# Two of a block's three split products as one product of 512 columns, and the halves added on VectorE

## What is computed

```
h = rmsnorm(x, g_mix)
(qa, ka, va, qb, kb, vb, qc, clat, iq, ik, iw, ga, gb, gc) = split(h @ w_in)
ya = swa_sink_attention(qa, ka, va)        # 16 heads
yb = moba_attention(qb, kb, vb)            # 8 heads
yc = dsa_attention(qc, rmsnorm(clat), ...) # 8 heads, 64 chosen keys
merged = (sigmoid(ga) * (ya @ w_br_a)
        + sigmoid(gb) * (yb @ w_br_b)
        + sigmoid(gc) * (yc @ w_br_c))
x = x + merged @ w_out
x = x + peer_ffn(rmsnorm(x, g_ffn), ...)
return rmsnorm(x, g_final)
```

## Time and profile before

| | |
|---|---|
| median of 3 runs | 2022.06 us (2021.14 to 2022.56) |
| profiled execution | 2017.58 us, its span 2016.3 us |
| TensorE matmul busy | 1781.4 us (88%) |
| VectorE busy | 1502.3 us (75%) |
| ScalarE busy | 924.2 us (46%) |
| GpSimd busy | 649.8 us (32%) |

### The profile page before, as it was taken

How to read it: one execution, slowest core, us unless ns; L and a number is a source line. 1 busy time by engine, 2 the same in 40 slices (tenths; PEclk the granted TensorE clock), 3 DMA queues, 4 the chain that set the end, 5 groups by cost and what they waited for, 6 DMA issues and landing times.

```text
span 2016.3 us, 28693 instructions
## 1 busy us (share of the span) xinstructions
PE 1781.4 (88%) x11068; PEld 1602.0 (79%) x11068; DVE 1502.3 (75%) x1986; ACT 924.2 (46%) x1474; POOL 649.8 (32%) x553
## 2 busy tenths in 40 slices
PE   6999999999999999957775244499999999999997
PEld 6999999999999887757775244488888888888886
DVE  4464444443466547998988899988988989999997
ACT  5444444444434441223443899843443443433443
POOL 1000000001035003467777677122222224435541
PEclk9999999999999999978988556799999999999999
DMA  9566565565555969999999999588999999999994
GB/s 312 172 173 170 164 173 171 165 176 164 159 168 201 341 208 416 371 419 402 417 412 419 371 389 400 212 333 350 407 415 386 401 398 398 403 414 404 403 407 193
DMA packets 293543, 627.88 MB, mean 311 GB/s; under 512 B 10364, under 2 KB 223405, under 8 KB 234958
## 3 DMA queue, kind: packets, MB, share of 16 engines
q0 software_dynamic: 48400, 343.95, 42.1%
q1 hardware_dynamic: 244414, 281.15, 40.6%
q10 hardware_dynamic: 640, 1.63, 0.2%
HBM read 622.45 MB, written 8.44 MB: 313 GB/s over the span
## 4 chain that ended last, share of the span: by engine, by line
PE 71%; DVE 10%; issue 5%; POOL 4%; ACT 4%; DMA 3%; DVEq 3%; POOLq 0%; ACTq 0%
PE ps L2043 34%; PE ps L1689 23%; DVE u_ring L1504 5%; PE ps L1885 4%; PE ps L1871 4%; DMA u_ring<-in_peer_u,idx_all 3%; DVEq L1454 3%; POOL u_ring L704 1%; POOL u_ring L713 1%; ACT ones L1141 1%; PE ps L1810 1%; PE ps L1791 1%; PE ps L2008 1%; POOL pick L723 1%; PE ps L1800 1%
## 5 line engine op out<-in xcount | busy, mean ns | idle before, releaser
L1263 DVE TENSOR_TENSOR w_lo<-raw,w_hi 128x2048 fp32r<-128x2048 f32 x111 | 256.8, 2313 | 319.4 <-ACT w_hi L787 319.4
L1689 PE MATMUL ps<-act_hi,w_hi 128*128 128x256 f32 x1520 | 436.9, 287 | 3.5 <-DVE act_lo L1387 2.9
L1689 PE MATMUL ps<-act_lo,w_hi 128*128 128x256 f32 x1520 | 430.8, 283 | 0.0
L1689 PE MATMUL ps<-act_hi,w_lo 128*128 128x256 f32 x1520 | 430.8, 283 | 0.0
L1198 ACT ACTIVATE v_hi<-v_raw 128x2048 fp32r<-128x2048 f32 x128 | 245.7, 1919 | 389.1 <-PE ps L2043 198.2
L2043 PE MATMUL ps<-v_hi,c_hi 128*128 128x512 f32 x1024 | 398.6, 389 | 1.2 <-DVE c_lo L1583 1.2
L2043 PE MATMUL ps<-v_lo,c_hi 128*128 128x512 f32 x1024 | 398.5, 389 | 0.0
L2043 PE MATMUL ps<-v_hi,c_lo 128*128 128x512 f32 x1024 | 398.5, 389 | 0.0
L1504 DVE CUSTOM_DVE_ANT_0 u_ring<-u_ring,ps 128x2048 f32<-128x2048 f32 x144 | 326.5, 2277 | 20.4 <-DMA u_ring<-in_peer_u,idx_all 20.1
L1579 DVE TENSOR_TENSOR v_lo<-v_raw,v_hi 128x2048 fp32r<-128x2048 f32 x128 | 293.2, 2291 | 53.2 <-ACT v_hi L1198 52.6
L787 ACT ACTIVATE w_hi<-raw 128x2048 fp32r<-128x2048 f32 x112 | 214.1, 1911 | 257.3 <-PE ps L1689 210.7
(11 more groups left out here) (253 smaller groups left out, 2297.8 us busy)
## 6 DMA issues: line engine op xcount, KB each, us to landing
v_raw<-in_peer_v SPq DMA_DIRECT2D x128, 1024.0 KB, 7.4
raw<-in_w_in SPq DMA_DIRECT2D x80, 1024.0 KB
raw<-in_w_out SPq DMA_DIRECT2D x16, 1024.0 KB
wq<-in_peer_w_q SPq DMA_DIRECT2D x8, 2048.0 KB, 13.3
raw<-in_w_br_a SPq DMA_DIRECT2D x16, 512.0 KB
bias_by_query<-bias_by_distance POOLq DMA_DIRECT2D x1, 4096.0 KB, 21.0
bias_st<-bias_by_query POOLq DMA_DIRECT2D x16, 256.0 KB, 4.7
raw<-in_w_br_b SPq DMA_DIRECT2D x16, 256.0 KB
```

What stands on the lines that cost most here:

```text
L1263: nc.vector.tensor_tensor(w_lo[:, j % NHL], raw[:, j % NRAW], w_hi[:, j % NHL].bitcast(F32), ALU.subtract).then_inc(lo_done, 1)
L1689: last = nc.tensor.matmul(out_ap, w_parts[wp][:, slot, k], act_parts[ap][:, k], start=(k == k0 and m == 0), stop=(k == k1 - 1 and m == 2))
```

## The change

High and low activations now lie in one tile `act_both` of shape [128, 2, 16, 256], and `act_hi` and `act_lo` are its halves. At each k the high weights multiply both halves in one matmul of 512 columns over a whole bank: its first 256 columns take high by high, its last 256 high by low. Low weights by high activations go, with 256 columns, into the first half. A block is 16 matmuls of 512 columns and 16 of 256. VectorE adds the halves of the bank: in the first stage and the bodies into a new tile `joined` (`join`), from which ScalarE then copies; in the merge the three sums of a block have a bank each (banks 0 to 2 or 3 to 5), and one `tensor_reduce` adds the halves of all three into `mtmp`, which one further instruction weights in place. TensorE now waits for `join_ok` in place of `evac_done`.

```
-                for m, (wp, ap) in enumerate(PRODUCTS):
-                    last = nc.tensor.matmul(out_ap, w_parts[wp][:, slot, k], act_parts[ap][:, k],
-                                            start=(k == k0 and m == 0), stop=(k == k1 - 1 and m == 2))
+            both, low_part = (w_hi[:, slot, k], act_both[:, :, k]), (w_lo[:, slot, k], act_hi[:, k])
+            pair = bank.rearrange("p (h t) -> p h t", h=2)
+            if k == k0:
+                nc.tensor.matmul(pair, *both, start=True, stop=False)
+                last = nc.tensor.matmul(bank[:, 0:T], *low_part, start=False, stop=False)
+            else:
+                nc.tensor.matmul(bank[:, 0:T], *low_part, start=False, stop=False)
+                last = nc.tensor.matmul(pair, *both, start=False, stop=(k == k1 - 1))
...
+        def join(n0, j):
+
+
+            dve.wait_ge(blk_done, n0 + (j + 1))
+            wait(dve, evac_done, n0 + (j - 1))
+            nc.vector.tensor_reduce(joined[:, j % 2], ps[:, J + j % 2].rearrange("p (h t) -> p t h", h=2), AX.X, ALU.add).then_inc(join_ok, 1)
...
-                act.wait_ge(blk_done, n0 + (j + 1))
-                nc.scalar.activation(gates[:, span(6 * T * b + T * (j - 2), T)], ps[:, J + j % 2, 0:T], ACT.Tanh,
+                act.wait_ge(join_ok, n0 + (j + 1))
+                nc.scalar.activation(gates[:, span(6 * T * b + T * (j - 2), T)], joined[:, j % 2], ACT.Tanh,
                                      scale=0.5).then_inc(evac_done, 1)
...
         for n in range(N_FIRST):
+            join(0, n)
             if n + 2 <= N_FIRST:
                 low(0, n + 2)
...
+            if not isinstance(b, int) or b > 0:
+                join(n0, -1)
             low(n0, 1)
+            join(n0, 0)
             low(n0, 2)
+            join(n0, 1)
             low(n0, 3)
             softmax(0)
+            join(n0, 2)
             low(n0, 4)
             softmax(1)
+            join(n0, 3)
             low(n0, 5)
+            join(n0, 4)
             low(n0, 6)
             outputs(0)
+            join(n0, 5)
             low(n0, 7)
             outputs(1)
+            join(n0, 6)
             low(n0, 8)
         dve.wait_ge(sink_in, 16)
         attention_bodies(dve, body)
+        join(N_BR, -1)
...
-                nc.vector.scalar_tensor_tensor(out=mtmp[:, j % 2, 0:2].rearrange("p g t -> p (g t)"), in0=gates[:, span(3 * T * m, 2 * T)],
-                                               scalar=1.0, in1=ps[:, J + j % 2, :], op0=ALU.add, op1=ALU.mult)
-                nc.vector.scalar_tensor_tensor(out=mtmp[:, j % 2, 2], in0=gates[:, span(3 * T * m + 2 * T, T)], scalar=1.0,
-                                               in1=ps[:, S_BANK + j % 2, 0:T], op0=ALU.add, op1=ALU.mult).then_inc(m_mul, 1)
+                nc.vector.tensor_reduce(mtmp[:, j % 2], ps[:, 3 * (j % 2):3 * (j % 2) + 3].rearrange("p g (h t) -> p g t h", h=2), AX.X, ALU.add)
+                dve.drain()
+                products = mtmp[:, j % 2].rearrange("p g t -> p (g t)")
+                nc.vector.scalar_tensor_tensor(out=products, in0=gates[:, span(3 * T * m, 3 * T)], scalar=1.0, in1=products,
+                                               op0=ALU.add, op1=ALU.mult).then_inc(m_mul, 1)
                 low(NRAW * i + N_BR, j + 2)
```

More of the change, by code:

```diff
@@ L230, in sem @@
         return ctx.enter_context(nc.semaphore(name))
-    act_hi = at("act_hi", 0, [P, NK, T], FR)
-    act_lo = at("act_lo", 16, [P, NK, T], FR)
+    act_both = at("act_both", 0, [P, 2, NK, T], FR)
+    act_hi, act_lo = act_both[:, 0], act_both[:, 1]
     w_hi = at("w_hi", 32, [P, NHL, NK, P], FR)
@@ L251, in build @@
     ident = at("ident", 204.5, [P, P])
+    joined = at("joined", 205, [P, 2, T])
     sinkb = at("sinkb", 207, [P, A_HEADS])
@@ L366, in build @@
     evac_done = sem("evac_done")
+    join_ok = sem("join_ok")
     SSQ = {0: 1, 1: 2, 2: 3, 4: 5, 5: 7}
@@ L839, in _ @@
                 high(0, n + 2)
-            bank = ps[:, J + n % 2]
+            bank = joined[:, n % 2]
+            act.wait_ge(join_ok, n + 1)
             if n in TURNED:
@@ L899, in queries @@
                 nc.scalar.activation(k_st[:, par], kT[:, span(key, T)], ACT.Copy)
-                act.wait_ge(blk_done, n0 + (par + 1))
-                nc.scalar.activation(q_st[:, par], ps[:, J + par, 0:T], ACT.Copy).then_inc(evac_done, 1)
+                act.wait_ge(join_ok, n0 + (par + 1))
+                nc.scalar.activation(q_st[:, par], joined[:, par], ACT.Copy).then_inc(evac_done, 1)
             def exps(par):
@@ L1681, in _, with wide_part, by_pairs @@
         w_wide = [w[:, :, :, :].rearrange("p s (a b) c -> p s a (b c)", b=WIDE // P) for w in w_parts]
-        def by_column(out_ap, slot, k0, k1, waits=None):
+        def wide_part(bank, slot, k, k0=0, k1=NK):
+            both, low_part = (w_hi[:, slot, k], act_both[:, :, k]), (w_lo[:, slot, k], act_hi[:, k])
[6 more added lines that the diff above has]
+                last = nc.tensor.matmul(pair, *both, start=False, stop=(k == k1 - 1))
+            return last
+        def by_pairs(bank, slot, k0=0, k1=NK, waits=None):
             for k in range(k0, k1):
@@ L1687, in by_column @@
                     waits(k)
-                for m, (wp, ap) in enumerate(PRODUCTS):
-                    last = nc.tensor.matmul(out_ap, w_parts[wp][:, slot, k], act_parts[ap][:, k],
-                                            start=(k == k0 and m == 0), stop=(k == k1 - 1 and m == 2))
+                last = wide_part(bank, slot, k, k0, k1)
             return last
@@ L1703, in first_part @@
             pe.wait_ge(xt_lo, k + 1)
-            for m, (wp, ap) in enumerate(PRODUCTS):
-                last = nc.tensor.matmul(ps[:, J, 0:T], w_parts[wp][:, 0, k], act_parts[ap][:, k], start=(k == 0 and m == 0), stop=(k == NK - 1 and m == 2))
-            return last
+            return wide_part(ps[:, J], 0, k)
         for k in range(NK):
@@ L1743, in _ @@
             pe.wait_ge(lo_done, n + 1)
-            wait(pe, evac_done, n - 1)
+            wait(pe, join_ok, n - 1)
             bank, slot = ps[:, J + n % 2], n % NHL
             if n:
-                by_column(bank[:, 0:T], slot, 0, NK).then_inc(blk_done, 1)
+                by_pairs(bank, slot).then_inc(blk_done, 1)
             if n - 1 in TURNED:
@@ L1780, in weights @@
                 pe.wait_ge(lo_done, n0 + (j + 1))
-                pe.wait_ge(evac_done, n0 + (j - 1))
-                by_column(ps[:, J + j % 2, 0:T], j % NHL, 0, NK).then_inc(blk_done, 1)
+                pe.wait_ge(join_ok, n0 + (j - 1))
+                by_pairs(ps[:, J + j % 2], j % NHL).then_inc(blk_done, 1)
             def scores(par):
@@ L1847, in merge @@
                     waits = lambda k: pe.wait_ge(y_lo, k // 4 + 1)
-                by_column(ps[:, J + j % 2, 0:T], j % NHL, 0, 8, waits)
-                by_column(ps[:, J + j % 2, T:2 * T], j % NHL, 8, 12, waits)
-                by_column(ps[:, S_BANK + j % 2, 0:T], j % NHL, 12, NK, waits).then_inc(blk_done, 1)
+                by_pairs(ps[:, 3 * (j % 2)], j % NHL, 0, 8, waits)
+                by_pairs(ps[:, 3 * (j % 2) + 1], j % NHL, 8, 12, waits)
+                by_pairs(ps[:, 3 * (j % 2) + 2], j % NHL, 12, NK, waits).then_inc(blk_done, 1)
         peeled(pe, NK // NRAW, merge)
```

## The result

The changed kernel takes 2048.03 us (median of 4 runs, 2045.08 to 2050.1) against 2021.6 us before (4 runs, 2020.91 to 2022.56): 1.0124 times the time before, 95% interval 1.0112 to 1.0136. The forecast was slower, 2037.7 us, with a range up to 2050. The profiled execution took 2047.76 us, its span 2046.5.

A forecast was written before the change was run, and what follows sets the result against it. TensorE was taken to bound up to 647 us, tied in the merge with the VectorE-GpSimd loop. Terms −2.9+0.7−13.1+0.9+0.8+27.5+1.7 = +15.6 us on 2022.06 gave 2037.7 us, range 2027 to 2050.

The forecast's parts named there:

- The merge, +27.5: Merge: steps of 7.5 us, adds waiting behind w_lo, 122.7 us instead of 95.2, so 27.5 us slower.
- The rival of the adds beside `w_lo`: Merge: GpSimd's adds run beside w_lo, step 5.55 us, total −16.9 us, 2005 us; chance 0.08.
- The rival with GpSimd's adds first: Merge: GpSimd's adds go before w_lo, step 6.95 us, 8 us less than forecast, 2029 us; chance 0.10.
- as the rival had it: Merge: TensorE's clock falls, blocks take 10.2 us or more, 45 us more for 16 blocks, 2082 us; chance 0.04.
- The clock at the product with w_out, +1.7: Behind the merge: TensorE idles some 7 us before the product with w_out, and a lower clock costs 1.7 us once.
- The joins of 0.69: VectorE: each join takes 0.69 us, and 80 of them cost TensorE nothing, with three exceptions.
- The part ahead of the merge, −13.6: First stage and bodies: the terms −2.9, +0.7, −13.1, +0.9 and +0.8 us together.
- a hidden wait of 1 us in each body: Bodies: rival that joins delay each of the 8 bodies by 1 us, 2045 us; chance 0.08.
- Blocks 1 to 14, −2.9: First stage: wide matmuls save 0.21 us in each of 14 blocks, 2.9 us faster.
- the join of block 15 stands among these rounds: +0.7 us: End of first stage: block 15's join, among VectorE's picking rounds, delays w_lo of block 17 by 0.7 us.
- The bodies, −13.1 and +0.9: Bodies: blocks 17 to 79 save 0.21 us each, 13.1 us; seven boundaries between bodies cost 0.9 us.
- The last gates, +0.8: Just ahead of the merge: the high activations wait for the last gates, 0.8 us slower.

The follow-up runs named there:

- adds-first kernel: Changed kernel with one more wait: in the merge VectorE starts w_lo only after GpSimd's two adds of the step; 2040.22 us, 1.0113 times the kernel before.
- deferred kernel: Changed kernel with mg_hi and mg_lo of each merge step made one step later, behind the next w_lo; 2022.42 us, 1.0019 times the kernel before.
- narrow kernel: Changed kernel with the wide matmul of the inner 14 of 16 steps k split into two of 256 columns; 2055.18 us, 1.017 times the kernel before.
- seam kernel: Changed kernel with a body's first w_hi made on ScalarE before the copy of the previous body's last gates; 2044.23 us, 1.0119 times the kernel before.
- best version: Changed kernel with old merge, join 15 earlier, a body's first w_hi before the gates' copy, last picking rounds behind body 0's first w_lo; 2014.04 us, 0.9962.

## Why the prediction was right, and where it was off

**The merge, +27.5: measured 27.3.** Sum 1.75, weighting 0.96, `w_lo` first, the first add waiting it out, the step 7.5: each as worked out. Between sum and weighting lie 0.17 us, where 0.08 had been taken, a term for which the prediction showed no row; and TensorE idles 1.1 to 2.0 us in 11 of the 15 steps, not 2 in each. The bound of the reduction that was taken (the rate of a weighting that reads PSUM) was the right one. That the excluded pair is the mechanism is shown by the adds-first kernel, that the order of waits makes it dear by the deferred one. The rival of the adds beside `w_lo` is out. The rival with GpSimd's adds first had its step at 6.95 us; where a wait enforces that order it is 7.18. The clock did fall inside the merge, against "so I count nothing there", but not for all 16 blocks as the rival had it: in two stretches of 5 us, at no cost in time.

**The clock at the product with w_out, +1.7: measured 1.8.**

**The joins of 0.69: measured 0.691, 80 of them.**

```profile
L1273 DVE TENSOR_REDUCE joined<-ps 128x256 f32<-128x512 f32 x80 | 55.3, 691 | 93.4 <-PE ps L1715 92.3
```

Before them VectorE waited 92.3 us for TensorE: they do stand in waits.

**The part ahead of the merge, −13.6: measured −3.6.** Here the prediction failed by 10 us, and its median of 2037.7 by the same. That 2048 still lay in the range, 2 us from its end, is in part luck: the range reached up to 2050 for a hidden wait of 1 us in each body, and what came was a handful of smaller things. Its steps:

- *Blocks 1 to 14, −2.9: −2.8 at `w_lo` 14* (120.26 for 123.04), but only in part by these blocks. From the start of block 1 to `w_lo` 14 are 90.62 us instead of 92.77, so the 14 blocks gave 2.15 us, 0.15 each and not 0.21. The other 0.6 us came because block 1 began at 29.64 instead of 30.27 us, for which nothing had been counted; in other executions of this code it began as late as 31.08.
- *The end of the first stage, "the join of block 15 stands among these rounds: +0.7 us".* I followed the join to the next `w_lo` and not to the other reader of its result, the copy `turn_st`, for which TensorE waits ahead of block 16. `w_lo` 17 is 0.55 us later than before where it should have been some 2.4 earlier, so 3 us were missed. By the execution of the deferred kernel, which had the same hole at full clock (21.1 us from `w_lo` 14 to 17), some 1.1 of them are the hole and 1.7 the fall of the clock behind it.
- *The bodies, −13.1 and +0.9.* From `w_lo` 17 to 78 the sum made 61 x 0.21 − 0.9 = −11.9 us; measured are 402.5 to 397.9, −4.6. Of the missing 7.3 us, the seams are 7 x 0.32 = 2.2: a stall of 0.45 instead of 0.13. I had set the time from the block's last matmul to the join as it was to the copy, but the last record is now a wide one, 0.39 for 0.28 us, so the join comes 0.11 later; and a copy of `joined` takes 0.42 where one from PSUM took 0.38. The pace, below, is 3.0: by the starts of their matmuls 30 of the 61 blocks take 5.65 and not 5.55 us. And three bodies (`w_lo` 25 to 49) take 52.2 us instead of 51.7. Ahead of their second set of transposes of the probabilities stands a wait for ScalarE that did not stand in the trace before. From the block's last matmul to these transposes pass 0.81, 0.65 and 0.68 us, 0.24 in the other bodies, together 1.4 us more:

```profile
317.03 0.85 PE L1831 MATMUL ps<-ident,probs 128*128 128x128 f32 x6 [0.28 <-ACT pT L921]
```

That sum, 2.2 + 3.0 + 1.4 = 6.6, leaves 0.7 us open.

- *The last gates, +0.8: measured 0.6*, from −4.1 us at `w_lo` 78 to −3.6 at the start of the merge.

"A body of 50.9 us": 51.7 and 52.2 were measured, 51.3 with the seam mended. The 0.21 us a block is therefore mis-sized as well: with the seam out of the way a body gains 1.2 us, 0.15 a block.

## What to carry to other kernels

When one engine is relieved by handing work to another, read what stands in the other's row in the tightest loop: here 0.1 to 0.2 us a block were bought with 1.75 us a step on an engine whose round had no slack at all, while the same trade cost little where that engine had waits. Of an inserted step, follow every reader of its result to the engine that you relieve, not only the next instruction in its own row. And a loop bound by a round over three engines is mended by moving the round one step later, at no cost in work: 24.6 us here.

## What the runs showed of the hardware that was not expected

**Two paces of the same matmuls.** Within one kernel, a step k of one matmul of 512 and one of 256 columns takes 0.347 us in some blocks and 0.353 in others. The wide matmuls in order of time, in two blocks of the changed kernel:

```profile
373.60 0.39 PE L1715 MATMUL ps<-act_both,w_hi 128*128 128x512 f32 x1
...
375.68 0.39 PE L1715 MATMUL ps<-act_both,w_hi 128*128 128x512 f32 x1
```

```profile
350.71 0.40 PE L1715 MATMUL ps<-act_both,w_hi 128*128 128x512 f32 x1
...
352.12 0.40 PE L1715 MATMUL ps<-act_both,w_hi 128*128 128x512 f32 x1
```

The first pair of starts is six steps apart, 2.08 us; the second four steps, 1.41 us. A block keeps its pace from end to end, with the clock at 1.00 in both. With 256 columns alone the pace is 0.12, before and in the narrow kernel. The order repeats: in the last three bodies of the seam kernel and of the best version, six bodies whose waits are alike, blocks 0, 2, 5 and 7 of each take 0.347 and blocks 1, 3, 4 and 6 take 0.353. So it seems to hang on what stands around a block, which no experiment varied by itself. What decides between the two stays open.

**The exclusion works in both directions.** VectorE's mg_lo was held back by an add of GpSimd that had itself been held back by VectorE: 0.96 instead of 0.43 us in the deferred kernel.

**The same hole, two clocks.** In the changed kernel TensorE idled 2.74 us from 124.3 and was granted 0.86 and 0.80 in the next two stretches of 5 us, that is 1.2 GHz for part of them. In the deferred kernel the same hole of 2.74 us, behind the same instructions, left it at 1.00 in both. In the merge of the changed kernel the clock stood at 1.00 with 1.50 and 1.64 us of idling (590 to 600), and it was 0.66 in the two stretches behind an idling of 2.01 us:

```profile
620.10 0.79 PE L1711 MATMUL ps<-act_both,w_hi 128*128 128x512 f32 x1 [2.01 <-DVE w_lo L1266]
650.45 0.49 PE L1711 MATMUL ps<-act_both,w_hi 128*128 128x512 f32 x1 [2.01 <-DVE w_lo L1266]
```

So the length of one idling alone does not tell whether the clock falls. A gain that hangs on the clock has to be read from several executions: between two of the same code it made 2.9 us here.
